# First attention scores ahead of the last projection tiles, head normalisation in two parts, and four smaller moves

## The chip, the cores and the metric

One core of one Trainium2 chip runs the whole program. The metric is the device time of one execution, in microseconds (us). All arithmetic is fp32. The core has TensorE (PE, matrix products and transposes), VectorE (DVE), ScalarE (ACT), GpSimd (POOL) and SyncE (SP), whose queue issues the loads of the weights. Each engine works through its own queue in order; a wait at the head of a queue holds back all that is queued behind it.

## The reference

A residual stream x of 256 tokens by 1024 channels goes through two blocks.

```python
def first_block(x, ...):            # two layers
    x = gated_post_add(x, swiglu_ffn(modulate_pre(x, ...), w_in, w_out), ...)      # 1024 -> 2 x 2816 -> 1024
    x = gated_post_add(x, short_conv_mixer(...) or nsa_mixer(...), ...)            # layer 0: conv, layer 1: nsa
    x = gated_post_add(x, swiglu_ffn(...), ...)

def second_block(x, c, ctx, c_ctx, ...):   # two layers, 256 tokens of x and, in layer 0, 256 of ctx beside them
    # layer 0: differential attention, 8 heads of 2 x 64, keys = ctx and x
    a = softmax(q1 k1) - lam * softmax(q2 k2);  o = rmsnorm(a @ v, subln) * 0.8;  y = o @ w_out
    x = x + g1 * y;  x = x + g2 * swiglu(modulate(rmsnorm(x), ...), w_gu, w_down)   # and the same for ctx
    # layer 1: grouped-query attention, 8 query heads, 2 key heads of 128, only x is carried on
```

A matrix product of fp32 numbers is made here of three products in a faster format: each operand is split into a high part (a copy, rounded) and a low part (what is left), and hi x hi, hi x lo and lo x hi are added in PSUM.

## The kernel before, in words

The program is a list of eleven stages, `subs` 0 to 10: ffn, conv, ffn, kv, ffn, nsa, ffn (256 tokens each), then diff (stage 7) and ffn (stage 8) with 512 tokens, gqa (stage 9, queries for 256 tokens, keys for 512) and ffn (stage 10, 256 tokens). Every engine has its program written out by hand, and semaphores tie them together: `t.done(ins, sem, label)` marks an instruction, `wait_ge(sem, t.at(label))` waits for it.

Weights stream in as units of 128 x 2048 (1 MB) through a ring of three. For each unit SP loads `stage`, ACT copies it to `w_hi` (`split`, L839), DVE subtracts to get `w_lo` (`split`, L1291). A stage has `units` for its first product and `bsteps` for its second, the `down` phase (L2104), in which PE makes all token tiles of one unit at a time, but tile by tile for the last two. The activations of the down phase lie in `mid` and are split piece by piece: piece j by ACT (`mid_split`, L864, marks `mhi_done`) and then by DVE (L1300, marks `mlo_done`), and PE's `ready(j)` waits for that and for the unit's `w_lo`. In the loop over the down steps ACT and DVE run `turn_over(j)`: `mid_split(j + 1)`, then `split` of the unit two ahead. In `nsa` and `gqa` PE writes the gate vector into two PSUM banks after its step 1 (`gate`, L2072), and ACT's copy of them (L1020) stands in `turn_over(0)`.

**diff and gqa** (`Wide`): the projection of 12 or 6 units goes through `rows_product` (L2181 to L2183), one 128-token tile at a time. ACT evacuates (L1119), squares (L1124) and takes roots (L1129) for the norms of q and k, DVE sums, scales and rotates them (L1698 to L1718), PE transposes the result two units later ("ut", L2371), and ACT evacuates that ("evu", L1137). A transposition i waits for evu i - 1, since both use banks 4 and 5. Then come the jobs of the attention (32 in diff, 16 in gqa): scores (L2388, L2391), the maximum on DVE (L1738, L1774, "neg"), the exponential on ACT (L1159, L1193, "exp"), scaling on DVE ("p"), transposition on PE (L2401, "jt"), evacuation on ACT, product with v on PE (L2415, L2418, "pv"). In diff, scores of job J go to banks 2 (J mod 2) and the next, and score J waits for exp J - 2.

**The end of diff**: after the last product ACT copies and squares the last head (L1170, L1174); DVE sums it, forms all 32 means, ACT takes one root over them (L1176), DVE one reciprocal (L1761) and scales the eight heads (L1766, "on"); PE transposes them (L2430, "ot"), ACT evacuates them to `mid` (L1180, "evo"), with `mid_split(0)` after head 3. The second half of the gate copies stands ahead of the eight heads.

**The context half of gqa**: the tokens 256 to 511 are needed from unit 4, tile 2 on. Their modulated activations are made in eight pairs of 128 x 256: DVE's `affine_pair` (L1456) from PSUM, ACT's `hi_pair` (L928), POOL's `lo_pair` (L801). DVE and ACT do all eight at unit 3 of the projection.

**The ffn with 512 tokens** (stage 8): the first piece of its down phase lies, as `h_hi` and `h_lo` slot 0, where chunks 0 and 1 of the up phase's activations were, so `mid_split(0)` waits for the end of the up phase, and PE's `down` waits for all of `mid`.

## Time and profile before

| | us |
|---|---|
| median of 3 runs | 2168.22 |
| lowest, highest | 2164.18, 2172.76 |
| profiled execution, its own time | 2161.73 |
| its span | 2160.0 |
| PE busy in the span | 2059.1 (95%) |
| DVE, ACT, POOL busy | 1380.7, 935.2, 102.5 |

The profiled execution lies 6.5 us below the median of the runs. "Granted clock" is the share of its full rate of 2.4 GHz that TensorE was given in a stretch; it shows two levels, 1.00 (2.4 GHz) and 0.50 (1.2 GHz). A row of the timeline gives start, duration, engine, line, operation and shapes; in brackets the idle time of the engine before it and who ended that.

### The profile page before, as it was taken

The numbers are of one execution on the slowest core, as the hardware profiler recorded it, in microseconds if no ns is written. First come the engines' busy times: TensorE is split into PE (matmuls) and PEld (weight loads), VectorE is DVE, ScalarE is ACT, GpSimd is POOL, SyncE is SP. The second block draws the span as 40 slices with busy tenths as digits, with TensorE's granted clock in tenths as the row PEclk, the third lists the DMA queues.
The fourth block names the chain that finished last, engine by engine and source line by source line (L and its number), as shares of the span: only waits on it lengthen the run. The fifth ranks groups of instructions, "written<-read, shape, count | busy, mean of one in ns | idle before, by whom it ended". The sixth has DMA issues, their size and how long they took to land.

```text
span 2160.0 us, 33553 instructions
## 1 busy us (share of the span) xinstructions
PE 2059.1 (95%) x13545; PEld 1820.7 (84%) x13545; DVE 1380.7 (64%) x1930; ACT 935.2 (43%) x1405; POOL 102.5 (5%) x150
## 2 busy tenths in 40 slices
PE   5999999999899999889999999999999999899999
PEld 3998898998799976459988997688888788868997
DVE  3768798687868784547865755857455335756444
ACT  4345435344633454444355435843222324454343
POOL 2000000000100001200001000010000001100000
PEclk8999999999999998999999999999999999999999
DMA  9897676887688856756855321024435232315553
GB/s 335 271 314 279 230 291 216 294 304 258 214 274 276 319 168 222 264 177 233 284 178 173 98 98 40 1 101 148 160 124 170 78 108 71 125 59 192 179 175 117
DMA packets 246616, 411.38 MB, mean 190 GB/s; under 512 B 10236, under 2 KB 191957, under 8 KB 246485
## 3 DMA queue, kind: packets, MB, share of 16 engines
q1 hardware_dynamic: 245888, 409.31, 55.2%
q8 instruction: 93, 1.52, 0.3%
q10 hardware_dynamic: 597, 0.23, 0.0%
q14 instruction: 38, 0.31, 0.0%
HBM read 408.47 MB, written 1.05 MB: 190 GB/s over the span
## 4 chain that ended last, share of the span: by engine, by line
PE 79%; DVE 9%; ACT 4%; DMA 4%; issue 2%; SPq 1%; POOL 1%; DVEq 0%; ACTq 0%
PE bank L2104 19%; PE bank L2004 14%; PE bank L2006 14%; PE bank L2005 14%; PE bank L2181 2%; PE bank L2183 2%; PE bank L2182 2%; DVE w_lo L1291 2%; DMA ada<-in_ada_w 2%; DVE gate_b L1338 1%; PE bank L1950 1%; DMA stage<-in_ffn_w_in 1%; ACT w_hi L839 1%; PE bank L1974 1%; PE bank L2388 1%
## 5 line engine op out<-in xcount | busy, mean ns | idle before, releaser
L1291 DVE TENSOR_TENSOR w_lo<-stage,w_hi 128x2048 fp32r<-128x2048 f32 x255 | 583.2, 2293 | 438.5 <-ACT w_hi L839 438.0
L839 ACT CAST w_hi<-stage 128x2048 fp32r<-128x2048 f32 x255 | 486.2, 1908 | 628.4 <-PE bank L2104 211.5
L2004 PE MATMUL bank<-h_hi,w_hi 128*128 128x256 f32 (+1 forms) x2336 | 698.1, 299 | 2.6 <-ACT mid L1035 2.6
L2005 PE MATMUL bank<-h_lo,w_hi 128*128 128x256 f32 (+1 forms) x2336 | 695.4, 298 | 0.0
L2006 PE MATMUL bank<-h_hi,w_lo 128*128 128x256 f32 (+1 forms) x2336 | 695.4, 298 | 0.0
L2004 PEld LDWEIGHTS bank<-h_hi,w_hi 128*128 128x128 f32 x2336 | 447.6, 192 | 16.0 <-issue 3.6
L2005 PEld LDWEIGHTS bank<-h_lo,w_hi 128*128 128x128 f32 x2336 | 447.7, 192 | 12.3
L2006 PEld LDWEIGHTS bank<-h_hi,w_lo 128*128 128x128 f32 x2336 | 447.4, 192 | 12.5
L2104 PE MATMUL bank<-w_hi,h_hi 128*128 128x512 f32 x776 | 244.9, 393 | 9.4 <-DVE h_lo L1300 7.9
L2104 PE MATMUL bank<-w_lo,h_hi 128*128 128x512 f32 x776 | 243.8, 391 | 0.0
L2104 PE MATMUL bank<-w_hi,h_lo 128*128 128x512 f32 x776 | 243.3, 391 | 0.0
L1338 DVE SCALAR_TENSOR_TENSOR gate_b<-ada,cond,gate_b 128x1024 f32<-128x1024 f32 x182 | 231.8, 1283 | 5.5
L2104 PEld LDWEIGHTS bank<-w_hi,h_hi 128*128 128x128 f32 x776 | 144.6, 189 | 41.4 <-issue 9.1
L2104 PEld LDWEIGHTS bank<-w_hi,h_lo 128*128 128x128 f32 x776 | 146.6, 189 | 30.8
L2104 PEld LDWEIGHTS bank<-w_lo,h_hi 128*128 128x128 f32 x776 | 146.4, 189 | 30.8
L2181 PE MATMUL bank<-w_hi,h_hi 128*128 128x256 f32 (+1 forms) x552 | 159.4, 289 | 7.5 <-POOL h_lo L801 6.2
L2183 PE MATMUL bank<-w_hi,h_lo 128*128 128x256 f32 (+1 forms) x552 | 157.8, 286 | 0.0
L2182 PE MATMUL bank<-w_lo,h_hi 128*128 128x256 f32 (+1 forms) x552 | 157.8, 286 | 0.0
L1234 ACT ACTIVATE silu_t<-bank 128x256 f32<-128x256 f32 (+1 forms) x132 | 53.2, 417 | 205.6 <-PE bank L2006 191.2
L1823 DVE TENSOR_TENSOR mid<-silu_t,bank 128x256 f32 (+3 forms) x132 | 60.4, 463 | 98.7 <-PE bank L2006 97.4
L2181 PEld LDWEIGHTS bank<-w_hi,h_hi 128*128 128x128 f32 x552 | 107.9, 196 | 8.2 <-POOL h_lo L801 6.7
L2182 PEld LDWEIGHTS bank<-w_lo,h_hi 128*128 128x128 f32 x552 | 108.0, 196 | 0.0
(256 smaller groups left out, 2019.8 us busy)
## 6 DMA issues: line engine op xcount, KB each, us to landing
ada<-in_ada_w SPq DMA_DIRECT2D x114, 1024.0 KB, 6.0
stage<-in_ffn_w_in SPq DMA_DIRECT2D x88, 1024.0 KB, 9.1
stage<-in_ffn_w_out SPq DMA_DIRECT2D x44, 1024.0 KB, 5.1
stage<-in_ffn_w_gu SPq DMA_DIRECT2D x44, 1024.0 KB, 5.2
stage<-in_ffn_w_down SPq DMA_DIRECT2D x22, 1024.0 KB, 5.0
stage<-in_a_w_in SPq DMA_DIRECT2D x12, 1024.0 KB, 7.9
stage<-in_diff_w_in SPq DMA_DIRECT2D x12, 1024.0 KB, 5.2
ada<-in_kv_ada_w SPq DMA_DIRECT2D x8, 1024.0 KB, 5.7
```

Of the source, the lines that this page charges most:

```text
L839: a.copy(w_hi[:, s, :], stage[:, s, :]).then_inc(hi_done, 1)
L1234: a.activation(silu_t[:, q, 0:T], bank[up_bank(s, j, i) + q][:, 0:T], ACT.Silu).then_inc(silu_done, 1)
L1291: v.tensor_tensor(w_lo[:, s, :], stage[:, s, :], w_hi[:, s, :].bitcast(F32), ALU.subtract).then_inc(lo_done, 1)
L1338: ins = v.scalar_tensor_tensor(out=acc[c], in0=w, scalar=cond[:, b, kk, c:c + 1], in1=acc[c], op0=ALU.mult, op1=ALU.add)
L1823: v.tensor_tensor(mid[:, bass.ds(o, T)], silu_t[:, q, 0:T], bank[up_bank(s, j, i) + 2 + q][:, 0:T], ALU.mult).then_inc(mid_done, 1)
L2004: m.matmul(dst[:, 0:T], wh, h_hi[:, h0:h0 + T], start=(k == ks[0]), stop=False)
L2005: m.matmul(dst[:, 0:T], wh, h_lo[:, h0:h0 + T], start=False, stop=False)
L2006: ins = m.matmul(dst[:, 0:T], wl, h_hi[:, h0:h0 + T], start=False, stop=(k == ks[-1]))
L2104: ins = m.matmul(y_bank(T, tt, h)[:, :], a_[:, r:r + P], w_[:, slot, kc * D + h * 512:kc * D + (h + 1) * 512], start=first and n == 0, sto ...
L2181: m.matmul(dst, h_hi[:, r], w_hi[:, slot, c], start=(k == ks[0]), stop=False)
L2182: m.matmul(dst, h_hi[:, r], w_lo[:, slot, c], start=False, stop=False)
L2183: ins = m.matmul(dst, h_lo[:, r], w_hi[:, slot, c], start=False, stop=(k == ks[-1]))
```

## The change

1. **nsa and gqa**: ACT's copies of the gate stand in `turn_over(1)`, behind `mid_split(2)` and the `split` of down unit 3.
2. **diff, start of the attention**: scores 0 and 1 stand ahead of the four tiles of the last projection unit, in banks 4 to 7 (`d_bank`), exps 0 and 1 ahead of its evacuations; scores 2 and 3 wait for no exp.
3. **diff, end**: heads 0 to 6 are summed, rooted and inverted ahead of head 7, whose own chain stands among the scalings. ACT's `mid_split(0)`, the second half of the gate copies and the root of head 7 stand ahead of evo 2.
4. **Stage 8**: ACT makes the first piece once PE has used chunk 1 in its last up product (mark "freed"), DVE makes it ahead of its last product; PE waits for all of `mid` only ahead of token tile 2.
5. **gqa, context half**: the eight affine pairs stand on ACT, three at unit 1, three at unit 2, two at unit 3, each followed by its hi_pair.
6. **gqa, start of the attention**: the last two transpositions ("ut" 3 and 4) stand ahead of tiles 1 and 2 of unit 5, scores 0 and 1 ahead of its tile 3, exps 0 and 1 ahead of ACT's evacuation of its second half.

The core of the diff:

```diff
+        def d_bank(J):
+            return 2 * (J % 2) + (4 if J < 2 else 0)
...
# ACT, mid_split
+                if s["T"] == 512 and s["kind"] == "ffn" and j == 0 and i is None:
+                    act.wait_ge(pe_s, t.at((f"s{s['n']}", "freed")))
+                    act.wait_ge(mid_done, s["c"] + 2)
+                elif s["T"] == 512 and s["kind"] == "ffn" and j == 1:
+                    act.wait_ge(w_used, u - 1)
+                    act.wait_ge(mid_done, s["c"] + 2 * s["bsteps"])
...
# ACT, late_pairs
+            def late_pairs(s, ks):
+
+                tag, c = f"s{s['n']}", s["cs"][1]
                 act.wait_ge(w_used, s["u"])
+                for k in ks:
+                    if pairs_late(s):
+                        for tt in (2 * c, 2 * c + 1):
+                            act.wait_ge(pe_s, t.at((tag, "tr", tt, k // 4)))
+                        act.wait_ge(pool_s, t.at((tag, "lo", k, s["cs"][0])))
+                        t.done(a.activation(h32_pair(k), xt_pair(c, k), ACT.Identity, scale=modc[:, s["A"], 8 * c + k:8 * c + k + 1],
+                                            bias=modv[:, mv(s, 0), 8 * c + k:8 * c + k + 1]), act_s, (tag, "h32", k, c))
+                    hi_pair(s, k, c)
...
# ACT, wide_act
+                        if w.diff and n == s["units"] - 1:
+                            diff_exp(tag, 0)
+                            diff_exp(tag, 1)
                         for half in halves:
+                            if not w.diff and n == 5:
+                                if half == 0:
+                                    turned(w.nk - 2)
+                                else:
+                                    turned(w.nk - 1)
+                                    gqa_exp(tag, 0)
+                                    gqa_exp(tag, 1)
...
-                            if n == 3 and pairs_late(s):
-                                late_pairs(s)
+                            if 0 < n < 4 and pairs_late(s):
+                                late_pairs(s, s["ks"][3 * n - 3:3 * n])
                             act.wait_ge(dve_s, t.at((tag, "rmean", n)))
...
# ACT, diff_act
+                    if J == len(jobs) + 1:
+                        root(0, 28)
...
-                act.wait_ge(dve_s, t.at((tag, "omean")))
-                t.done(a.activation(ada_row[:, 64:96], ada_row[:, 32:64], ACT.Sqrt, scale=1.0 / P), act_s, (tag, "oroot"))
-                gate(s, tag, 1)
                 for h in range(8):
+                    if h == 2:
+                        mid_split(s, 0)
+                        gate(s, tag, 1)
+                        root(28, 32)
                     act.wait_ge(pe_s, t.at((tag, "ot", h)))
                     t.done(a.activation(mid[:, h * 512:(h + 1) * 512], bank[h % 4][:, :], ACT.Copy, scale=SUBLN), act_s, (tag, "evo", h))
-                    if h == 3:
-                        mid_split(s, 0)
...
# ACT, turn_over
-                    if j == 0 and i is None and s["kind"] in ("nsa", "gqa"):
+                    if j == 1 and i is None and s["kind"] in ("nsa", "gqa"):
                         gate(s, tag, 0)
...
# DVE, wide_dve and diff_dve
-                    if n == 3 and pairs_late(s):
-                        late_pairs(s)
...
+                means(0, 28)
+                inverses(0, 28)
                 for h in range(8):
+                    if h == 4:
+                        osum(7)
+                        means(28, 32)
+                    if h == 7:
+                        inverses(28, 32)
...
# DVE, last step of the up phase
+                            if q and j == 10 and T == 512:
+                                mid_split(s, 0)
...
# PE, down
-                if T == 512 and s["kind"] == "ffn":
-                    pe.wait_ge(mid_done, s["c"] + 2 * s["bsteps"])
...
+                        if s["kind"] == "ffn" and T == 512 and i is None and j == 0 and tt == 2:
+                            pe.wait_ge(mid_done, s["c"] + 2 * nb)
...
# PE, wide_pe
+                        if w.diff and n == s["units"] - 1:
+                            pe.wait_ge(act_s, t.at((tag, "evu", w.nk - 1)))
+                            scores(0)
+                            scores(1)
                         for tt in order:
                             half = tt // 2
+                            if not w.diff and n == 5:
+                                if tt in (1, 2):
+                                    turned(w.nk - 3 + tt)
+                                if tt == 3:
+                                    pe.wait_ge(act_s, t.at((tag, "ev", 4, 1)))
+                                    pe.wait_ge(act_s, t.at((tag, "evu", w.nk - 1)))
+                                    scores(0)
+                                    scores(1)
...
-                    if 0 <= i < w.nk:
+                    if 0 <= i < (w.nk if w.diff else w.nk - 2):
+                        turned(i)
...
-                        if J >= 2:
+                    if 2 <= J < len(jobs):
+                        if not w.diff or J >= 4:
                             pe.wait_ge(act_s, t.at((tag, "exp", J - 2)))
```

`turned(i)` is the transposition of unit i (on PE) or its evacuation (on ACT), moved into a function; `scores`, `diff_exp`, `gqa_exp`, `root`, `means` and `inverses` hold what stood in the loops before.

## Rows read from the trace of the kernel before

**Rows 1.** The page, part 4: the chain that ended last, by engine.

```profile
PE 79%; DVE 9%; ACT 4%; DMA 4%; issue 2%; SPq 1%; POOL 1%; DVEq 0%; ACTq 0%
```

**Rows 2.** Waits of PE, whole span: us in total, times, longest us.

```profile
PE bank L2104 <- DVE h_lo L1300: 7.9, 5, 2.5
PE bank L2181 <- POOL h_lo L801: 6.2, 2, 5.7
```

**Rows 3.** Timeline of PE, gates, stage 8, diff and gqa: start us, us.

```profile
956.56 0.70 PE L2104 MATMUL bank<-w_hi,h_hi 128*128 128x512 f32 x2 [2.06 <-DVE h_lo L1300]
960.57 0.70 PE L2104 MATMUL bank<-w_hi,h_hi 128*128 128x512 f32 x2 [1.04 <-DVE h_lo L1300]
...
1321.95 1.99 PE L2388 MATMUL bank<-mid,ada 64*128 64x512 f32 x8 [0.72 <-ACT mid L1119]
1325.88 0.70 PE L2388 MATMUL bank<-mid,ada 64*128 64x256 f32 x4 [1.94 <-ACT gate_b L1159]
...
1397.10 6.64 PE L2430 MATMUL bank<-ident,ada 128*128 128x128 f32 x32 [2.88 <-DVE ada L1766]
...
1702.87 0.70 PE L2104 MATMUL bank<-w_hi,h_hi 128*128 128x512 f32 x2 [2.48 <-DVE h_lo L1300]
...
1891.90 1.12 PE L2391 MATMUL bank<-mid 128*128 128x512 f32 x2 [0.92 <-ACT mid L1193]
...
1942.09 0.85 PE L2104 MATMUL bank<-w_hi,h_hi 128*128 128x512 f32 x2 [2.13 <-DVE h_lo L1300]
```

**Rows 4.** Busy time by stretch: length, PE, PEld, DVE, ACT, POOL, granted clock, DMA, GB/s.

```profile
955.00:962.00 7.00, 4.40 (x18) 3.41 (x19) 5.17 (x5) 4.82 (x5) 0.00 (x0) 1.00 0.63 240
1328.00:1331.40 3.40, 3.40 (x11) 1.51 (x11) 2.62 (x6) 2.33 (x9) 0.00 (x0) 0.51 0.00 0
1396.50:1403.00 6.50, 5.90 (x28) 5.93 (x29) 5.23 (x9) 4.58 (x8) 0.00 (x0) 0.50 0.00 0
1703.50:1706.90 3.40, 3.40 (x10) 2.62 (x9) 2.37 (x2) 3.17 (x3) 0.00 (x0) 0.51 0.03 7
1864.00:1870.60 6.60, 5.81 (x27) 5.81 (x28) 6.00 (x15) 0.38 (x1) 0.73 (x1) 0.50 0.00 0
1942.60:1945.90 3.30, 3.30 (x9) 2.55 (x9) 2.92 (x4) 2.66 (x3) 0.00 (x0) 0.50 0.32 127
```

**Rows 5.** The same view over the stretches of the gqa projection.

```profile
1864.80:1873.20 8.40, 8.40 (x48) 8.40 (x49) 5.20 (x14) 0.00 (x0) 0.00 (x0) 0.64 0.25 66
1873.60:1885.20 11.60, 11.60 (x99) 11.60 (x98) 7.68 (x10) 5.18 (x8) 0.00 (x0) 1.00 0.07 29
```

**Rows 6.** Timeline of ACT and DVE in gqa.

```profile
1851.80 0.21 ACT L1129 ACTIVATE astat<-astat 128x4 f32<-128x4 f32 x1 [3.09 <-DVE astat L1700]
...
1877.80 0.63 ACT L1137 COPY mid<-bank 128x256 f32<-128x256 f32 x2
...
1881.42 0.69 DVE L1718 TENSOR_TENSOR mid<-silu_t 128x512 f32<-128x512 f32 x1
```

**Rows 7.** One line's instructions: ns minimum/median/maximum, first and last start us.

```profile
L1063 ACT ACTIVATE mid<-bank,q_scale x8: 473/475/476, 807.0 to 826.6; 128x256 f32<-128x256 f32 x8
L928 ACT CAST h_hi<-mid x48: 391/407/411, 1123.7 to 1860.9; 128x256 fp32r<-128x256 f32 x48
L1300 DVE TENSOR_TENSOR h_lo<-mid,h_hi x82: 681/685/1226, 168.5 to 2142.8; 128x512 fp32r<-128x512 f32 x67, 128x1024 fp32r<-128x1024 f32 x15
L1433 DVE TENSOR_TENSOR h_lo<-mid,h_hi x6: 1455/1457/1459, 241.6 to 1960.6; 128x512 fp32r<-128x512 f32 x6
L793 POOL TENSOR_TENSOR h_lo<-mid,h_hi x53: 450/732/2774, 35.7 to 1965.2; 128x256 fp32r<-128x256 f32 x27, 128x128 fp32r<-128x128 f32 x18, 128x512 fp32r<-128x512 f32 x8
```

**Rows 8.** Timeline of ACT at the end of diff.

```profile
1394.01 0.63 ACT L1174 ACTIVATE silu_t<-ada 128x512 f32<-128x512 f32 x1
...
1395.75 1.06 ACT L1020 COPY gate_b<-bank 128x512 f32<-128x512 f32 x2
...
1401.37 1.04 ACT L864 CAST h_hi<-mid 128x1024 fp32r<-128x1024 f32 x1
```

More of the change, by code:

```diff
@@ L1099, in wide_act, with turned @@
                 w, u = Wide(s), s["u"]
+                def turned(i):
+                    act.wait_ge(pe_s, t.at((tag, "ut", i)))
+                    for c in range(2):
+                        k = w.tiles(i) * P
+                        if w.diff and i == 0 and c == 0:
+                            act.wait_ge(*ring_free(rv(s["v"] - 1) * VEC_UNITS + 3))
+                        ins = a.copy(w.dest(i, c), bank[4 + c][:, 0:k])
+                    t.done(ins, act_s, (tag, "evu", i))
                 if w.diff:
@@ L1130, in wide_act @@
                     i = n - 2
-                    if 0 <= i < w.nk:
-                        act.wait_ge(pe_s, t.at((tag, "ut", i)))
-                        for c in range(2):
-                            k = w.tiles(i) * P
-                            if w.diff and i == 0 and c == 0:
-                                act.wait_ge(*ring_free(rv(s["v"] - 1) * VEC_UNITS + 3))
-                            ins = a.copy(w.dest(i, c), bank[4 + c][:, 0:k])
-                        t.done(ins, act_s, (tag, "evu", i))
+                    if 0 <= i < (w.nk if w.diff else w.nk - 2):
+                        turned(i)
                 if w.diff:
@@ L1902, in _ @@
                     wide_dve(s, tag)
-                if s["kind"] in ("diff", "gqa") or T == 512:
+                if s["kind"] in ("diff", "gqa"):
                     mid_split(s, 0)
@@ L1975, in acc_sum, with cols_product @@
                 ins.then_inc(ada_sum, 1)
-            def cols_product(s, dst, slot, q, first=False):
+            def cols_product(s, dst, slot, q, first=False, last=False):
                 T, ks = s["T"], s["ks"]
@@ L2006, in cols_product @@
                     ins = m.matmul(dst[:, 0:T], wl, h_hi[:, h0:h0 + T], start=False, stop=(k == ks[-1]))
+                    if last and k == 1:
+                        t.done(ins, pe_s, (f"s{s['n']}", "freed"))
                 return ins
@@ L2332, in wide_pe, with turned, scores @@
                 w, u = Wide(s), s["u"]
+                def turned(i):
+                    pe.wait_ge(dve_s, t.at((tag, "rope", i)))
+                    if i:
+                        pe.wait_ge(act_s, t.at((tag, "evu", i - 1)))
+                    for c in range(2):
+                        for tt in range(w.tiles(i)):
+                            o = tt * WCOL + c * P
+                            ins = m.transpose(bank[4 + c][:, tt * P:(tt + 1) * P], w.nat(i)[:, o:o + P], ident[:, :])
+                    t.done(ins, pe_s, (tag, "ut", i))
+                def scores(J):
+                    h, tt, k0 = jobs[J]
+                    if w.diff:
+                        for m_ in range(2):
+                            r = slice(64 * m_, 64 * m_ + 64)
+                            ins = m.matmul(bank[d_bank(J) + m_][:, 0:(4 - k0) * P], w.qT[r, h, tt * P:(tt + 1) * P],
+                                           w.kT[r, h, k0 * P:512], start=True, stop=True)
+                    else:
+                        ins = m.matmul(bank[J % 2][:, :], w.qT[:, h, tt * P:(tt + 1) * P], w.kT[:, h // 4, :], start=True, stop=True)
+                    t.done(ins, pe_s, (tag, "s", J))
+                jobs = diff_jobs if w.diff else gqa_jobs
                 def context_part(n):
@@ L2363, in wide_pe @@
                     i = n - 2
-                    if 0 <= i < w.nk:
-                        pe.wait_ge(dve_s, t.at((tag, "rope", i)))
-                        if i:
-                            pe.wait_ge(act_s, t.at((tag, "evu", i - 1)))
-                        for c in range(2):
-                            for tt in range(w.tiles(i)):
-                                o = tt * WCOL + c * P
-                                ins = m.transpose(bank[4 + c][:, tt * P:(tt + 1) * P], w.nat(i)[:, o:o + P], ident[:, :])
-                        t.done(ins, pe_s, (tag, "ut", i))
+                    if 0 <= i < (w.nk if w.diff else w.nk - 2):
+                        turned(i)
                 n = s["units"] - 1
@@ L2481, in up_step @@
                                     pe.wait_ge(mid_done, c + 2 * (j - 1) + q + 1)
-                            ins = cols_product(s, bank[banks[part] + q], n % RING, q, first and part == 0 and q == 0)
+                            ins = cols_product(s, bank[banks[part] + q], n % RING, q, first and part == 0 and q == 0,
+                                               s["kind"] == "ffn" and T == 512 and i is None and j == 10 and part == 1 and q == 1)
                             ins.then_inc(w_used if q else part_done[part], 1)
```

86 lines of the change are left out of this document (40 added, 46 removed).

## Prediction

> **What bounds the kernel now.** The chain of the page comes first: 79% of it is PE's [rows 1], and PE is busy for 95% of the span. So a microsecond counts only where PE stands still, or runs at the lower clock, and the change has to be read at those places. PE's waits are read next, with the timeline of PE for the time of each [rows 2, 3]: the reader is to see six gaps at the places that the change touches, 2.06 and 1.04 us behind the gate of nsa, 0.72 and 1.94 us at the start of diff's attention, 2.88 us ahead of the transpositions that end diff, 2.48 us between up and down phase of stage 8, 5.7 us in the projection of gqa, 2.13 us behind the gate of gqa. Third, the busy time by stretch [rows 4]: behind five of these places PE has a granted clock of 0.50 (the 1.2 GHz level) for 3.3 to 6.6 us, though it is busy. Only behind the 2.06 us of nsa the clock stayed at 1.00. A gap of over 2 us thus mostly costs about half of such a stretch on top of itself.
>
> **The change part by part.** The terms are savings of PE time, against the profiled execution's own 2161.7 us.
>
> *Gate copies (1).* In turn_over(0) ACT waited for PE's gate, and behind that wait in its queue stood mid_split 2, which PE needs first after the gate, and the split of unit 3. With the copies one turn later, piece 2 and w_hi, w_lo of unit 3 are made while PE is still in steps 0 and 1 (11 us), and only piece 3 (0.6 us on ACT, 0.69 us on DVE) stands behind the copies; PE needs it after twelve products of 512 columns, 2.8 us at twice the 0.12 us of a product of 256 (96 of them took 11.6 us [rows 5]), so it is hidden. What is queued behind the moved copies is that piece alone; the gate itself is read by the residual update, after the down phase. SP issues nothing new; its next load waits for w_lo of unit 3 and starts earlier. nsa: 2.06 + 1.04 = 3.1 us [rows 3] (2.1 if the second gap stays). gqa: 2.13 us, and half of the 3.3 us at clock 0.50 behind it [rows 3, 4], 1.65: 3.8 us (2.1 without the clock).
>
> *Start of diff's attention (2).* Scores 0 and 1 cost 1.9 us of PE before and after [rows 3], so moving them is free. Their maxima and exps (about 5 us of DVE and ACT) fall into unit 11, 11.6 us of PE as unit 5 of gqa [rows 5], in which both engines are nearly idle. After the unit PE waits 0.72 us for its evacuation as before, then runs scores 2 and 3. Unit 11 ended at 1321.2; with the scores it ends at 1323.1, score 2 starts at 1323.8 instead of 1325.88 [rows 3]: 2.1 us. Then the stretch at clock 0.51 [rows 4], which followed the gap of 1.94 us: it can go with the gap. A job waits for DVE and ACT too, so between nothing and half of the 3.4 us, 1.7, is to be had; PE is busy for all of the stretch, which is nearer to the upper end, and I take 1.1. Sum 3.2 us, from 1.9 to 3.8.
>
> *End of diff (3).* DVE can scale heads 0 to 3 from about 1392.5 on. PE's heads 0 and 1 follow the gate at 1394.2. But head 2 goes into a bank of the second gate half, and ACT now copies that half behind evo 0, evo 1 and mid_split 0. From the end of the last square at 1394.64 [rows 8]: two evos 0.6 + 0.6 with 0.2 of handing over, the piece 1.04, the copies 1.06: 1398.2. PE so waits 3.1 us between heads 1 and 2, where it waited 2.88 us before head 0 [rows 3]. The clock then most likely falls as it did [rows 4], and the six heads left take 6.64 / 8 = 0.83 us each [rows 3], to 1403.2, with DVE's first piece long done; before, the down phase started at 1403.8. That is 0.6 us, and up to 0.5 us of the down phase falls into the low stretch: I take 0.3 us. At full clock heads 2 to 7 would be bound by ACT (0.6 each) and end at 1400.8: 3.0 us. The bounds are -0.5 and 3.0.
>
> *First piece of stage 8 (4).* ACT's copy (1.04) and DVE's subtraction (1.23 [rows 7]) fit in the 18 products of 0.23 us, 4.2 us, that are left after chunk 1; both engines idle there. DVE's last product stands behind its piece and is not late, since it waits for PE's end anyway. Saved: 2.48 us [rows 3] and half of 3.4 us [rows 4], 1.7: 4.2 us (2.5 without the clock). Piece 1 still waits for the end of the up phase; it takes ACT and DVE under 4 us, while step 0 is 11 us of PE: hidden. The wait for all of mid ahead of tile 2 comes 5.5 us into it.
>
> *Context half of gqa (5).* The 5.7 us wait for POOL's last piece [rows 2] goes, if POOL is done when PE comes to tile 2 of unit 4, at 1858.9. One pair on ACT is 0.475 + 0.407 us [rows 7]. Three pairs are 2.65 us, two 1.8 us, and ACT idled 3.09 us ahead of its root, at unit 1 and again at unit 2 [rows 6]: hidden. At unit 3 the two pairs end at 1857.4, POOL 0.7 to 1.5 us later, about when PE comes. Without the wait the second half of unit 4 also runs at full clock: 48 products took 8.40 us, while 96 take 11.6 in unit 5 [rows 5], so 5.8: 2.6 us. Together 8.3 us at the end of unit 4. DVE loses eight operations and gains an overlap: POOL's pieces now meet w_lo subtractions. A DVE subtraction beside a POOL one took 1.457 instead of 0.685 us, and a POOL one up to 2.77 us instead of 0.73 [rows 7]: one waits for the other. Each of three meetings costs DVE from nothing to 0.8 us; PE stands 0.5 us from needing DVE's results. I take 0.6 us off: 7.7 us; the bounds are 4 and 8.3.
>
> The Trainium skill, GPSIMD Engine Reference, section Key points, says that GpSimd shares its SBUF interfaces with VectorE and contends with VectorE instructions that have two SBUF inputs. By that rule the pieces speak against this place, and the trace agrees in kind (the 1.457 us). If each of the eight pieces held DVE up for all of its 0.73 us, an estimate of 5.8 us, gqa would give 2 us here and the forecast would be 2150.
>
> *Start of gqa's attention (6).* Count from the end of unit 4, 1873.2 before [rows 5]. PE's tile 0 of unit 5 ends at +3.3 with the transposition before it. Transposition 3 must wait for evu 2, which stands in ACT's queue behind the root of unit 4: it ended at 1878.43 [rows 6], +5.2. A new stall of 1.9 us. Transposition 3 (0.4) and tile 1 (2.9) end at +8.5; transposition 4 needs DVE's rotation, done at 1882.1 [rows 6], +8.9; with it (0.9), tile 2, two scores (0.9), tile 3 PE is at +16.5, and score 2 follows the evacuation at +17.2. Before it started at 1891.90 [rows 3], +18.7. Gain 1.5 us; if the clock falls after the 1.9 us, as it did after 1.94 us, -0.2 us or less, -1.8 at worst.
>
> Sum: 3.1 + 3.8 + 3.2 + 0.3 + 4.2 + 7.7 + 1.5 = **23.8 us**, 1.1%. On the profiled execution that gives 2137.9. The median of the runs lies 6.5 us higher, and I take the saving off that: **2144 us**. All terms at their low end give 2.1 + 2.1 + 1.9 - 0.5 + 2.5 + 4 - 1.8 = 10.3, at their high end 3.1 + 3.8 + 3.8 + 3.0 + 4.2 + 8.3 + 1.5 = 27.7.
>
> **The rivals.**
> *A, DVE and POOL in each other's way.* If DVE loses 1 us at unit 1 and another at unit 2, ACT's root and so evu 0 come 2.3 us late, PE waits ahead of transposition 1, and a low stretch (1.7 us) follows: gqa's term falls from 9.2 to about 4. For it: the 1.457 us. Against: POOL took the longer waits in the rows. Saving 18 us: 2150.
> *B, the clock stays up at the end of diff.* Gap 3.1 against 2.88 speaks against it. Saving 26.5: 2142.
> *C, the time is given back further on.* If the loads of the 256-token ffn stages paced them, an earlier start would end in a wait for weights. PE has no wait for a load behind nsa at all, so little speaks for it. Only the last three places would count in part; saving under 10 us: 2160.
> *D, slower: the low clock over the attentions.* New, shorter gaps could keep PE low through diff's 75 us and gqa's 37 us of attention. By my value the stretch of 3.4 us cost 1.1 us, 0.33 per us: 37 us for 112, less the 23.8: 2181. It decides from about 105 us of low clock on. Against it: the trace has no other low stretch in either attention, and they have fewer gaps afterwards.
>
> **How the numbers follow.** About 0.5% (10.8 us) is what a measurement of this kernel can tell from no change. The forecast's own case has a chance of 0.70 (2138 to 2150), A 0.14, B 0.07, C 0.05, D 0.04. Faster: 0.70 + 0.14 + 0.07, less some executions that lie high: 0.89. Same 0.07, slower 0.04. The range takes in A, B and the ends of the costs: from 2161.7 - 27.7 to 2168.2 - 10.3, that is 2134 to 2158.
>
> **What would show it.** Right: no wait for POOL in gqa and clock 1.00 over units 4 and 5; no gap between up and down phase of stage 8, and none behind the gates; a gap of about 3 us between heads 1 and 2 at the end of diff, and one of about 2 us in unit 5 of gqa. Wrong: a wait ahead of transposition 1 of gqa, POOL pieces or w_lo subtractions there well over their usual length, clock 0.50 in new places, a wait for weights in the stage behind.

## The result, and the profile of the changed kernel

| | before | changed |
|---|---|---|
| median of 3 runs, us | 2168.22 | 2140.71 |
| lowest, highest, us | 2164.18, 2172.76 | 2136.26, 2147.65 |
| profiled execution, its own time, us | 2161.73 | 2147.65 |

The ratio is 0.9873, with a 95% interval of 0.983 to 0.9915: faster by 27.5 us, where 2144 (2134 to 2158) was forecast. Two later series of the changed kernel, experiments e7b and e11 below, gave 0.9901 (0.9881 to 0.9921) and 0.9901 (0.9881 to 0.9922). The median of its 13 executions is 2144.84 us.

The chain of the page, by engine, now has more of PE and no POOL (before: [rows 1]).

```profile
PE 80%; DVE 10%; ACT 4%; DMA 3%; issue 2%; SPq 1%; POOL 0%; DVEq 0%; ACTq 0%
```

Of PE's waits by line and releaser (us in total, times, longest), two are new. Those of [rows 2] are gone but for 0.2 us on DVE and 0.5 us on POOL, neither at a place of the six edits. The new ones:

```profile
PE bank L2398 <- ACT mid L1123: 3.3, 2, 1.8
...
PE bank L2505 <- ACT gate_b L1036: 3.0, 1, 3.0
```

PE's timeline at the places of [rows 3], in the changed kernel (start, duration, operation, idle time before it and its releaser):

```profile
963.86 1.03 PE L2130 MATMUL bank<-ident,modc 128*128 128x128 f32 x8
964.65 0.70 PE L2160 MATMUL bank<-w_hi,h_hi 128*128 128x512 f32 x2
...
1316.73 1.99 PE L2406 MATMUL bank<-mid,ada 64*128 64x512 f32 x8
...
1331.19 1.13 PE L2406 MATMUL bank<-mid,ada 64*128 64x256 f32 x8 [0.77 <-ACT mid L1155]
1333.73 1.13 PE L2406 MATMUL bank<-mid,ada 64*128 64x512 f32 x4 [0.82 <-ACT mid L1182]
...
1401.77 4.20 PE L2505 MATMUL bank<-ident,ada 128*128 128x128 f32 x24 [3.02 <-ACT gate_b L1036]
1405.62 1.10 PE L2160 MATMUL bank<-w_hi,h_hi 128*128 128x512 f32 x2
...
1702.14 0.39 PE L2062 MATMUL bank<-h_hi,w_lo 128*128 128x512 f32 x1
1702.37 0.62 PE L2160 MATMUL bank<-w_hi,h_hi 128*128 128x512 f32 x2
...
1851.50 0.63 PE L2398 MATMUL bank<-ident,mid 128*128 128x128 f32 x4 [1.52 <-ACT mid L1123]
...
1868.77 0.63 PE L2398 MATMUL bank<-ident,mid 128*128 128x128 f32 x4 [1.82 <-ACT mid L1123]
1872.37 1.09 PE L2398 MATMUL bank<-ident,mid 128*128 128x128 f32 x8
1876.17 1.88 PE L2409 MATMUL bank<-mid 128*128 128x512 f32 x4
1881.64 1.10 PE L2409 MATMUL bank<-mid 128*128 128x512 f32 x2 [0.72 <-ACT mid L1155]
...
1928.63 1.03 PE L2130 MATMUL bank<-ident,modv 128*128 128x128 f32 x8
1929.42 0.70 PE L2160 MATMUL bank<-w_hi,h_hi 128*128 128x512 f32 x2
```

The reader is to see the first product of the down phase right behind the gate's transpositions (L2130) in nsa and gqa, and right behind the last product of the up phase (L2062) in stage 8; the 3.02 us gap, now between heads 1 and 2 at the end of diff; and in gqa no wait on POOL, but 1.52 us ahead of transposition 1 and 1.82 us ahead of transposition 3. The busy time by stretch (columns as [rows 4]) shows the clock at 1.00 at these places, but for the end of diff and the last row, a stretch of nsa's attention that no edit touches:

```profile
964.60:971.60 7.00, 7.00 (x34) 5.80 (x33) 3.71 (x5) 4.56 (x8) 0.00 (x0) 1.00 1.04 384
1333.00:1336.40 3.40, 2.67 (x18) 1.79 (x20) 3.31 (x7) 2.81 (x11) 0.00 (x0) 1.00 0.00 0
1402.70:1406.30 3.60, 3.60 (x20) 3.50 (x19) 1.19 (x2) 3.27 (x6) 0.00 (x0) 0.55 0.02 5
1851.00:1867.00 16.00, 15.45 (x128) 15.27 (x128) 13.76 (x27) 9.70 (x16) 2.31 (x3) 1.00 0.39 143
1868.70:1872.10 3.40, 3.33 (x28) 3.32 (x28) 3.33 (x6) 2.27 (x3) 0.00 (x0) 1.00 0.12 43
1926.00:1934.00 8.00, 8.00 (x41) 6.71 (x40) 3.76 (x4) 3.40 (x4) 0.00 (x0) 1.00 1.04 393
...
912.00:921.00 9.00, 9.00 (x44) 5.30 (x40) 3.02 (x22) 2.29 (x10) 1.82 (x2) 0.50 0.39 133
```

To place the time, I cut each trace at waits of PE that every kernel here has: m1, the wait of 2.3 us at the boundary ahead of nsa's kv stage (798 us); m2, the 4.0 us at the boundary behind nsa (974 in before); m3, the 1.47 us at 1122; m4, the 1.20 us ahead of the last pair of products of diff's attention (1390); m5, the 0.65 us at the boundary behind diff (1457); m6, score 2 of gqa (1892); m7, the 2.15 us at the boundary behind gqa (1960). Lengths in us, each from one profiled execution:

| kernel | own time | m1-m2 | m3-m4 | m4-m5 | m5-m6 | m6-m7 |
|---|---|---|---|---|---|---|
| before | 2161.73 | 175.64 | 267.83 | 67.06 | 434.63 | 68.14 |
| before, again (e12) | 2173.78 | 184.53 | 268.92 | 66.92 | 433.48 | 67.75 |
| changed | 2147.65 | 182.60 | 264.69 | 65.56 | 422.23 | 64.11 |
| changed, again (e7b) | 2144.55 | 177.53 | 264.49 | 63.91 | 423.40 | 64.13 |
| changed, again (e11) | 2141.41 | 176.73 | 264.36 | 63.92 | 422.23 | 64.11 |
| four places put back (e1) | 2154.47 | 175.98 | 268.96 | 63.92 | 427.82 | 68.09 |
| two further edits (e8b) | 2140.00 | 174.68 | 264.27 | 62.96 | 421.40 | 64.12 |
| three further edits (e10) | 2137.95 | 174.92 | 264.55 | 62.98 | 420.39 | 64.11 |

The two first profiles differ by 14.1 us, not 24: between m1 and m2 the changed one is 7.0 us longer, though its gate there costs 3.6 us less (from the gate's transpositions to m2 17.12 us, before 20.70). The other 10.5 us are low clock in nsa's attention: over m1-m2 the granted clock was 0.82 on average, in before 0.88, and PE was busy for 164.6 us instead of 154.6.

### The profile page after: what moved, and what is told of

Its sections match the earlier page's. It is cut to its first block, busy times and chain, and to the rows that moved or that the text cites. A ratio compares the mean times of both kernels' runs of the same rounds, so it can differ in the third digit from the quotient of the medians.

```text
span 2145.9 us, 33562 instructions
## 1 busy us (share of the span) xinstructions
PE 2060.0 (96%) x13545; PEld 1820.0 (85%) x13545; DVE 1377.7 (64%) x1925; ACT 939.0 (44%) x1414; POOL 104.6 (5%) x150
## 3 DMA queue, kind: packets, MB, share of 16 engines
q8 instruction: 93, 1.52, 0.3%
HBM read 408.47 MB, written 1.05 MB: 191 GB/s over the span
## 4 chain that ended last, share of the span: by engine, by line
PE 80%; DVE 10%; ACT 4%; DMA 3%; issue 2%; SPq 1%; POOL 0%; DVEq 0%; ACTq 0%
PE bank L2160 19%; PE bank L2060 14%; PE bank L2062 14%; PE bank L2061 14%; PE bank L2239 2%; PE bank L2241 2%; PE bank L2240 2%; DVE w_lo L1335 2%; DVE gate_b L1382 1%; PE bank L2006 1%; DMA ada<-in_ada_w 1%; DMA xs<-in_ada_w 1%; PE bank L2030 1%; ACT w_hi L842 1%; PE bank L2406 1%
## 5 line engine op out<-in xcount | busy, mean ns | idle before, releaser
L2062 PE MATMUL bank<-h_hi,w_lo 128*128 128x256 f32 (+1 forms) x2336 | 695.4, 298 | 0.0
L2062 PEld LDWEIGHTS bank<-h_hi,w_lo 128*128 128x128 f32 x2336 | 447.4, 192 | 12.5
```

Of the source, the lines that this page charges most:

```text
L2062: ins = m.matmul(dst[:, 0:T], wl, h_hi[:, h0:h0 + T], start=False, stop=(k == ks[-1]))
```

## The experiments

**Is each part worth what its place shows?** e1 puts four places back; of its edit, the gates and the order of stage 8 and of diff's scores:

```
-                    if j == 1 and i is None and s["kind"] in ("nsa", "gqa"):   # ACT: gate copies
+                    if j == 0 and i is None and s["kind"] in ("nsa", "gqa"):
...
-                            if q and j == 10 and T == 512:                       # DVE: first piece of stage 8
-                                mid_split(s, 0)
...
-                        if w.diff and n == s["units"] - 1:                       # PE, ACT: scores 0, 1 early
-                            scores(0)
-                            scores(1)
```

> The changed kernel with four of its places put back as they were: the gate copies of nsa and of gqa at turn-over 0, the start of diff's attention (scores 0 and 1 behind the last unit), and the first piece of stage 8 behind the last product. The end of diff and both gqa projection parts stay. Theory (each part is worth what its own place shows, independent of the others): against the changed kernel the marks of the trace fall back by 3.6 us at the gate of nsa, 3.1 at the start of diff's attention, 4.4 at stage 8 and 4.0 at the gate of gqa, 15 us together; the gaps of 2.06 and 1.04, of 1.94, of 2.48 and of 2.13 us stand there again, and the low clock behind three of them. Rival (what one place gives another takes back, or the places share their low clock): under 10 us together. A second question: the stretch of nsa's attention, which no part touches, had more low clock in the changed kernel's profile (10 us longer). If that comes with the changed program it is here too; if it comes with the single execution, this profile may have it or not.

One execution took 2154.47 us. All four gaps stand there again (2.06 and 1.03, 1.94, 2.49, 2.13 us). Two of them:

```profile
1702.32 0.70 PE L2151 MATMUL bank<-w_hi,h_hi 128*128 128x512 f32 x2 [2.49 <-DVE h_lo L1335]
...
1934.68 0.70 PE L2151 MATMUL bank<-w_hi,h_hi 128*128 128x512 f32 x2 [2.13 <-DVE h_lo L1335]
```

From the gate to m2 it needs 20.73 us, 3.6 more than the changed kernel. The start of diff (m3-m4) costs 4.3 us, more than the 3.1 by which the first profiles differ: the low clock behind the gap lasts 6.8 us here, as in e12, instead of 3.4 [rows 4]. Stage 8 costs 4.4 (m5 to the first transposition of gqa: 388.59 against 384.22) and the gate of gqa 4.0 (m6-m7). Together 16.3 us against the 15 expected: what these four places give is not taken back at another. All four were undone at once, none of them alone. The rest of m5-m6, 1.2 us, is a stretch of low clock behind the 1.82 us gap of gqa, which the changed kernel's first profile does not have. The stretch of nsa is a short one in this execution, 175.98 us with the old place of the gate copies.

**What holds DVE in gqa?** In the changed kernel DVE's round per unit is 6.85 us where it was 6.31, and evacuation 0 so comes 1.1 us later. DVE and POOL there:

```profile
1840.13 2.29 DVE L1335 TENSOR_TENSOR w_lo<-stage,w_hi 128x2048 fp32r<-128x2048 f32 x1
1842.33 0.68 DVE L1740 TENSOR_REDUCE astat<-mid 128x4 f32<-128x512 f32 x1
1843.04 0.69 DVE L1742 TENSOR_SCALAR astat<-astat 128x4 f32<-128x4 f32 x1
...
1846.99 2.29 DVE L1335 TENSOR_TENSOR w_lo<-stage,w_hi 128x2048 fp32r<-128x2048 f32 x1
```

```profile
1841.12 1.89 POOL L804 TENSOR_TENSOR h_lo<-mid,h_hi 128x256 fp32r<-128x256 f32 x1 [13.90 <-ACT h_hi L937]
...
1842.97 1.42 POOL L804 TENSOR_TENSOR h_lo<-mid,h_hi 128x256 fp32r<-128x256 f32 x2
```

The scaling of four elements took 0.69 us, where it takes 0.17 elsewhere. It ran beside POOL's second piece and ended 0.02 us behind it (the two of the last row start at 1842.97; the second piece ends at 1843.71). POOL's first piece took 1.89 us instead of 0.73: it began inside w_lo and ended 0.6 us after it. e2 cuts POOL's pieces to 16 of their 256 columns and leaves the rest of these low parts out:

```
-                t.done(g.tensor_tensor(dst, h32_pair(k), hi, ALU.subtract), pool_s, (tag, "lo", k, c))
+                src = h32_pair(k)
+                if pairs_late(s) and c == s["cs"][1]:
+                    dst, src, hi = dst[:, :, 0:8], src[:, :, 0:8], hi[:, :, 0:8]
+                t.done(g.tensor_tensor(dst, src, hi, ALU.subtract), pool_s, (tag, "lo", k, c))
```

> The changed kernel, but each of POOL's eight late subtractions in gqa covers 16 of its 256 columns; the rest of the context half's low parts is left out. It asks what made DVE's period per unit 6.85 instead of 6.31 us. Theory A (POOL's pieces hold DVE): the small scaling of four elements, 0.69 us beside POOL, takes 0.17 again, DVE's period is 6.3 us, and the wait of PE ahead of transposition 1 falls from 1.52 to about 0.5 us: 1.0 us less. Rival (ACT's late pairs delay the root): DVE's period stays at 6.8 us and the wait at 1.5 us, since ACT's work is the same.

Its scaling, over all of the kernel (ns minimum/median/maximum):

```profile
L1745 DVE TENSOR_SCALAR astat<-astat x13: 170/174/175, 1205.4 to 1868.6; 128x16 f32<-128x16 f32 x8, 128x4 f32<-128x4 f32 x4, 128x8 f32<-128x8 f32 x1
```

The round is 6.30 us and the wait ahead of transposition 1 is 0.45 us, 1.07 less (before had 0.46); m5-m6 is 421.18, 1.05 shorter. ACT's work is the same, so it is POOL that holds DVE. e3 takes DVE's scaling away instead, in gqa alone:

```
...
+                            else:
+                                t.done(a.activation(flat_astat[:, 32:32 + k], flat_astat[:, 0:k], ACT.Sqrt, scale=1.0 / P, bias=stat[:, 31:32]), act_s, (tag, "rroot", n))
...
+                        if w.diff:
+                            dve.wait_ge(dve_s, t.at((tag, "rsum", n)))
+                            t.done(v.tensor_scalar(flat_astat[:, 16:16 + k], flat_astat[:, 0:k], 1.0 / dh, EPS, ALU.mult, ALU.add), dve_s, (tag, "rmean", n))
```

> The changed kernel, but in gqa the root takes the scale and the added constant itself (as its scale and bias), so that DVE's scaling of the means, the one operation that grew from 0.17 to 0.69 us beside POOL, is gone. Theory 1 (the loss sits in that one operation): DVE's period falls from 6.85 to about 6.1 us and PE's wait ahead of transposition 1 to 0.3 us or less, 1.2 us or more saved. Theory 2 (whatever DVE does beside POOL's piece is held up): the next operation takes over the 0.5 us, the period is about 6.6 us, the wait about 1.1 us, 0.4 us saved.

```profile
1830.32 0.69 DVE L1754 TENSOR_TENSOR mid<-mid,astat 128x512 f32<-128x512 f32 x1
1831.04 1.12 DVE L1762 TENSOR_TENSOR silu_t<-mid,gate_b 128x512 f32<-128x512 f32 x1
1832.08 0.41 DVE L1763 TENSOR_TENSOR silu_t<-mid,gate_b 128x256 f32<-128x256 f32 x1
```

Theory 2 in kind: a later operation of the round now loses 0.43 us (1.12 instead of 0.69) and the round is 6.61 us. But the loss has moved behind the root, so evacuation 0 is not held: the wait is 0.54 us, 0.98 less, where theory 2 expected a wait of 1.1 us, and m5-m6 is 0.9 us shorter (421.37). This kernel's execution took 2133.30 us, that of e4 below 2149.80, with at most 1 us between their edits: 13.5 of the 16.5 us lie between m1 and m2.

**Was it the spreading or the engine?** e6b spreads the eight scale-and-shift operations as the change does, but leaves them on DVE:

```
...
+                    if 0 < n < 4 and pairs_late(s):                      # DVE, ahead of the sums of unit n
+                        for kk in s["ks"][3 * n - 3:3 * n]:
+                            affine_pair(s, kk, s["cs"][1])
```

> The changed kernel, but the eight scale-and-shift operations of gqa's context half, spread over units 1 to 3 as 3, 3 and 2, are done on DVE as before, 0.46 us each, ahead of each unit's sums. It asks whether the spreading alone gives the gain, or the engine. Theory (ACT had room and DVE had none): DVE's period at units 1 and 2 grows from 6.85 to about 8.2 us, PE's wait ahead of transposition 1 from 1.52 to about 2.9 us, another wait of 1 us or more ahead of transposition 2, perhaps low clock behind it: gqa's projection takes 2.5 to 5 us longer than in the changed kernel. Rival (the spreading is what counts): within 0.7 us of the changed kernel there.

```profile
1851.79 1.08 PE L2395 MATMUL bank<-ident,mid 128*128 128x128 f32 x4 [3.82 <-ACT mid L1117]
```

DVE's round is 8.03 us, the wait 3.82 us, and the clock is at 0.50 from 1849.9 to 1856.6. The second wait that was expected, ahead of transposition 2, is not there, but m5-m6 is 4.5 us longer (426.74). Spreading alone gives less than half of the 7.5 us; the rest needs the idle ACT.

**The wait in unit 5 of gqa.** e4 takes ACT's queue away as its cause:

```
+                            if not w.diff and n == 4:
+                                turned(2)                                 # ACT, ahead of the root
                             act.wait_ge(dve_s, t.at((tag, "rmean", n)))
```

> The changed kernel, but in gqa ACT copies out transposition 2 ahead of the root of unit 4, in the 1.49 us in which it waits for DVE. Theory (ACT's queue is only the first of two reasons): the wait of 1.82 us ahead of transposition 3 goes down to 0.3 us or less, but transposition 4 needs DVE's rotation of unit 4, and PE now waits 1.5 to 2 us for that ahead of tile 2: nothing saved (within 0.3 us). Rival (the queue was the bound): 1.5 us saved, no new wait on DVE.

```profile
1869.66 0.63 PE L2400 MATMUL bank<-ident,mid 128*128 128x128 f32 x4
...
1874.96 1.09 PE L2400 MATMUL bank<-ident,mid 128*128 128x128 f32 x8 [1.80 <-DVE mid L1762]
```

The 1.82 us ahead of transposition 3 are gone and 1.80 us stand ahead of transposition 4; m5-m6 is 422.24, in the changed kernel 422.23. Nothing is saved. So the chain through DVE has to be shortened, which e9 does:

```
+                            if n == 4 and tt == 3 and not w.diff:
+                                turned(2)                                 # PE, inside unit 4
...
+                            if not w.diff and n == 4 and half == 0:       # ACT: square of the first half
+                                a.activation(w.sq[:, 0:512], w.nat(4)[:, 0:512], ACT.Square)
```

> The changed kernel, but in gqa transposition 2 stands ahead of tile 3 of unit 4 instead of behind the unit, its evacuation ahead of that of unit 4, and ACT squares unit 4 in two halves, so that the first half is copied and squared while PE is still in tile 3. Experiment e4 put the bound of unit 5 at DVE's rotation of unit 4, which follows the square. Theory (the chain ACT copy, square, DVE sums and rotation of unit 4 is the bound): the square ends about 1.1 us earlier, counted from the end of unit 4, the wait of 1.82 us ahead of transposition 3 is gone, a wait of about 0.7 us on DVE stands ahead of transposition 4, and score 2 comes 1.1 us earlier (0.7 to 1.5). Rival (transposition 2 stalls PE inside unit 4, since evacuation 1 or rotation 2 is late there): a new wait of over 0.5 us inside unit 4 takes the gain back.

```profile
1858.14 0.60 PE L2405 MATMUL bank<-ident,mid 128*128 128x128 f32 x4
...
1868.93 1.09 PE L2405 MATMUL bank<-ident,mid 128*128 128x128 f32 x8 [1.14 <-DVE mid L1767]
```

Transposition 2 does not wait inside unit 4, the wait on DVE is 1.14 us (0.7 was expected), and from transposition 1 to score 2 there are 29.16 us instead of 30.14: 0.98 saved.

**The gap at the end of diff.** e5b changes the order on ACT:

```
+                gate(s, tag, 1)
                 for h in range(8):
                     if h == 2:
+                        root(28, 32)
                         mid_split(s, 0)
-                        gate(s, tag, 1)
-                        root(28, 32)
```

> The changed kernel, but at the end of diff ACT copies the second gate half ahead of evo 0 and 1, and takes the root of head 7 and the first piece behind them. Theory (the 3.02 us gap between heads 1 and 2 is ACT's order alone): the bank of head 2 is free at about the end of the last square plus 1.1 us, the gap falls to 0.6 to 0.8 us, DVE's first piece ends the wait of the down phase, and the down phase starts 2.1 us earlier (1.5 to 2.5), with up to 0.5 us more if the low clock behind the gap goes too. Rival (what follows is bound elsewhere: eight evos on ACT at 0.63 us or the scaling on DVE): the gap goes, but the down phase starts less than 0.7 us earlier, with new waits of PE between heads 4 and 7.

```profile
1398.23 2.15 PE L2505 MATMUL bank<-ident,ada 128*128 128x128 f32 x16 [0.55 <-ACT gate_b L1036]
1401.21 1.21 PE L2505 MATMUL bank<-ident,ada 128*128 128x128 f32 x8 [0.83 <-DVE ada L1820]
1402.37 0.70 PE L2160 MATMUL bank<-w_hi,h_hi 128*128 128x512 f32 x2
```

From m4 to the down phase it takes 9.58 us. That is 2.2 less than the 11.77 of the changed kernel's first profile, but that one has low clock there; against e7b and e11, which like e5b have none, it is 0.9 less (10.51), not the 2.1 of the theory. Head 2 starts 2.5 us earlier, and 1.5 of them are lost again: from head 2 to the down phase it takes 4.14 us instead of 2.60, with a new wait of 0.83 us ahead of head 6. The rival expected such a wait, but less than 0.7 us of gain; the result lies between the two. m4-m5 is 62.95: 2.6 us less than in the first profile, 1.0 less than in those of e7b and e11.

The row puts the new wait down to DVE. But DVE had scaled head 6 by 1400.27, and in the program head 6 also waits for evacuation 2, whose bank it takes. That one stood in ACT's queue behind the first piece and ended at 1401.07, 0.02 us ahead of DVE's last scaling (head 7), which the row names:

```profile
1399.44 1.05 ACT L873 CAST h_hi<-mid 128x1024 fp32r<-128x1024 f32 x1
1400.39 0.68 ACT L1231 ACTIVATE mid<-bank,stat 128x512 f32<-128x512 f32 x1
...
1400.40 0.69 DVE L1820 TENSOR_TENSOR ada<-ada,ada_row 128x512 f32<-128x512 f32 x1
```

So it is again ACT's order, as read from the program and these rows; no run moved the piece.

**Times, and the stretch of nsa.** e7b is the changed kernel again, e8b has the edits of e3 and e5b, e10 those and the edit of e9, e11 is the changed kernel beside e10, e12 the kernel before.

> The changed kernel as it is, timed again beside the kernel before. Theory (the parts' marks add up to 24.5 us, and the rest of what one profile shows is the clock over nsa's attention, which differs between executions): ratio 0.9887 (24.5 of 2168), within 0.984 to 0.992. Rival (the median of the first runs, 27.5 us, is the size): 0.987 or less with an interval that leaves 0.9887 out. The profile's marks from 1130 us on lie as in the first profile within 1 us once the start of the stretch is subtracted; only the stretch of nsa's attention and the low clock behind boundaries may differ.

Measured: 2146.31 us (2144.55 to 2148.86), ratio 0.9901 (0.9881 to 0.9921). The interval holds the theory's 0.9887, so the rival falls.

> The changed kernel with two further edits: the gate copies first at the end of diff, and the root of gqa with its scale and constant on ACT, so that DVE's small scaling beside POOL's pieces is gone. Theory (both waits were real and lie at separate places): 2.1 + 1.0 = 3 us less than the changed kernel, a ratio against the kernel before lower by 0.0014; the interval of the times can't resolve that, the marks of the trace can: down phase of diff 2.1 us earlier, transposition 1 of gqa 1.0 us earlier. Rival (the gain is given back at the next boundary): the marks behind gqa lie less than 1.5 us earlier, reckoned from the start of diff.

Measured: 2139.11 us (2134.72 to 2140.00), ratio 0.9857 (0.9837 to 0.9878). The marks give 0.96 us between m4 and m5 against e7b, 2.6 against the first profile of the changed kernel, and 0.8 between m5 and m6 (against 422.23). Where the clock stays up, the two edits together are thus worth 1.8 us, not the 3 expected. The times differ by 7.2 us, more than the marks explain.

> The changed kernel with three further edits together: gate copies first at the end of diff, the root of gqa with scale and constant on ACT, transposition 2 of gqa ahead of tile 3 of unit 4. Theory (separate places, all of it on PE's path): 2.1 to 2.6 at the end of diff, 0.9 and 1.1 in gqa, 4.1 to 4.6 us less than the changed kernel, a ratio to the kernel before of about 0.9875 if the changed kernel's is 0.9895. Rival (the low clock over nsa's attention decides more than that): the two intervals of this call overlap, though the marks show the 4 us.

Measured: 2137.95 us (2131.71 to 2140.58), ratio 0.9854 (0.9832 to 0.9877). m5-m6 is 420.39, 1.84 shorter, just the 0.86 of e3 and the 0.98 of e9 together. m4-m5 is 62.98, 0.9 shorter than in e11, where 2.1 to 2.6 were expected. The three edits thus give 2.8 us by the marks, not 4.1 to 4.6; the medians differ by 8.4. This version has the lowest median here, and its interval lies just below that of the changed kernel:

> The changed kernel as it is, on the same chip as the run before, to have both against the same runs of the kernel before. Theory: ratio 0.989 (0.987 to 0.991); where the end of diff shows no low clock, the stretch from the last pair of products to the boundary is 63.9 us long, where it does, 65.6; the same for 12.9 or 14.1 us from transposition 3 to the third score of gqa.

Measured: 2146.31 us (2140.08 to 2149.72), ratio 0.9901 (0.9881 to 0.9922). Its profile has no low clock at either place, with 63.92 us and 12.87 us from transposition 3 to score 2, as expected for that case.

> The kernel before as it is, for a second profile of it. The stretch from the start to the end of nsa's attention and down phase (between two fixed marks at about 798 and 974 us) took 175.6 us in its first profile, and 170.4 to 183.8 us in eleven profiles with the gate copies moved, where 172.0 would answer to the first profile (3.6 us less for the gate). Theory (executions differ there, whatever the kernel, and the first profile of before was a short one, as its own time, 6.5 us under the median, says): the profiled time less that stretch is again 1986 us within 2 us, however long the stretch is, and it is more likely longer (median of the other profiles 177.8 plus 3.6, 181 us) than 176. Rival (moving the gate copies itself lengthens nsa's attention by some 6 us): the stretch is 174 to 177 us again, and the profiled time near 2162 us, far from the kernel's median of 2168.

Measured: 2173.78 us; the stretch m1-m2 took 184.53, so the rival, which had it at 174 to 177 again, falls. What is left of the time is 1989.3 us, 3.2 more than in the first profile and 1.3 more than the theory allowed: 1.3 us lie ahead of m1, 1.4 between m2 and m3, 1.1 in the longer low clock between m3 and m4, and others of opposite sign behind them. With 3.6 us off for the gate, the two profiles of before have 172.0 and 180.9 us between m1 and m2; the eleven with the gate copies moved have 170.4 to 183.8. So a lengthening by 6 us is not seen. One of a few us is not ruled out: only three profiles have the old place of the copies (e1's stretch is 172.4 us on the same count).

## Why the prediction was right, point by point

| term | forecast (bounds), us | measured, us |
|---|---|---|
| gate of nsa | 3.1 (2.1 to 3.1) | 3.6 |
| gate of gqa | 3.8 (2.1 to 3.8) | 4.0 (3.6 against e12) |
| start of diff | 3.2 (1.9 to 3.8) | 3.1; 4.2 to 4.6 against e12 and e1 |
| end of diff | 0.3 (-0.5 to 3.0) | 1.5; 3.1 where the clock stays up |
| stage 8 | 4.2 (2.5 to 4.2) | 4.4 |
| gqa, context half | 7.7 (4 to 8.3) | 7.5 (6.4 against e12) |
| gqa, start of attention | 1.5 (-1.8 to 1.5) | 0.5; -0.7 where the clock falls |
| sum | 23.8 (10.3 to 27.7) | 24.6 |

The measured column is the difference of the first two profiles, cut at the marks; e1 confirms four of its rows by undoing them. The median of 13 executions lies 23.4 us under the first median of before. The 27.5 us of the first three runs are 3 us more than the marks, the 21.8 and 22.8 us of the medians of e7b and e11 2 to 3 us less; the kernel's executions differ by 13.5 us among themselves. That the sum of the marks is only 0.8 us off the forecast is in part luck: 1.2 us too little at the end of diff, 0.9 too little at the gates and stage 8, 1.0 too much at the start of gqa's attention and 0.2 in its context half.

*Gates.* Right in mechanism, 0.5 us short in nsa. Two gaps of 3.10 us cost 3.58, 0.24 each beside the idle time. An estimate from the rows gives the same: the pairs of products in the down phase follow each other every 0.46 us while each record lasts 0.62, so a gap reckoned from a record's end is 0.16 too short; and the first pair behind a gap takes 0.70, 0.08 more. The forecast took only idle time and clock, so nsa, gqa (4.0) and stage 8 (4.4) all lie above their upper bounds. Piece 3 behind the moved copies was hidden, as the clock of 1.00 and a busy PE from 964.6 to 971.6 show.

*Start of diff.* Right in mechanism; the sum is right because two errors cancel. Score 2 was to start 2.1 us earlier; counted from m3 it starts 1.5 us earlier (203.50 to 202.03 us; 1.8 in e11). The clock's share was taken as 1.1 us of a 3.4 us stretch, but from score 2 to m4 the time fell from 64.33 to 62.66 us, 1.7 less, half of the stretch. Where that stretch is 6.8 us long, as in e1 and e12, it is worth about 1 us more.

*End of diff.* The gap came out as worked out (3.02 for 3.1 us). The step that failed was that the clock falls "as it did", with 0.83 us for each of heads 2 to 7. It fell 1.3 us after they began and stayed down for 3.4 us, where it had been down for 6.8 in before, so that they took 3.85 us and not 6 times 0.83. Rival B, which had the clock stay up there and 3.0 us saved, is the case of three of nine profiles with this gap (e1, e7b, e11), and 3.1 us are saved there. The price is right, its working is not: at ACT's 0.6 us each the six heads would have ended at 1401.8 in the forecast's own count, not at 1400.8, and only 2.0 us would have been saved. In e11 they take 2.60 us, 0.43 each, and no wait for ACT stands among them:

```profile
1397.62 2.84 PE L2505 MATMUL bank<-ident,ada 128*128 128x128 f32 x24 [3.02 <-ACT gate_b L1036]
1400.21 0.71 PE L2160 MATMUL bank<-w_hi,h_hi 128*128 128x512 f32 x2
```

*Stage 8.* Right, gap and clock: 2.48 + 1.9 us.

*Context half of gqa.* The sum is right to 0.2 us, and its shape too, a little gained and a little lost. Rival A was right in its place (a wait ahead of transposition 1, DVE late) and wrong in its price: 0.54 us per round and 1.1 us for PE by unit 1, not 2.3, and no low clock behind it. The forecast had 0.6 us off for it. The short operation, not the long one, was held: w_lo kept its 2.29 us, and the price was paid by the scaling of four elements behind it. The Trainium skill (GPSIMD Engine Reference, Key points) puts the contention at instructions of VectorE in a 2-port performance mode or with two SBUF inputs; e2 bears out that the engines hold each other; the held scaling has one input, and whether it ran in such a mode no run shows. By that rule each of POOL's eight pieces could have cost its 0.73 us, where a burst of three cost 0.54 once.

*Start of gqa's attention.* The 1.82 us (1.9 forecast) ahead of transposition 3 and the time of transposition 4 (9.0 us behind the end of unit 4, forecast 8.9) came out. The step that failed is the cost of the two scores: 0.9 us was set down for both, and each costs 0.94 ([rows 3] has 1.12 with its tail for one). That is the missing 1.0 us. The fall of the clock behind the wait (1.7 to 1.8 us), set as possible, came in two of ten profiles (e1, e7b) and cost 1.2 us.

*C and D.* C is out: no wait for a weight stands behind nsa, and with the stretch m1-m2 set aside m7 lies earlier by the full sum (21.1 us from m2 on, and 3.6 for the gate of nsa). D is out: neither attention has new low stretches but those named, and diff's attention takes 62.66 us from score 2 to m4 in every profile with the early scores, within 0.05 us.

*The range* held, but not for the reason given. It was made of costs and bounds of the edits; the spread that showed is in nsa's attention, where PE waits for loads and for the other engines and the clock falls behind some waits and not others. Both profiles of before came from the two ends of that spread (2161.73 and 2173.78). Setting the saving off against the median, not the profiled execution, was right for that reason.

What stays open: why the clock falls behind the same wait in one execution and not in another. The runs show only that it is not the kernel (three profiles of the changed one differ in it), and what a fall costs at each place. And of the 7.2 us by which e8b is faster than e7b, only 1.8 to 3.4 have a place in the marks.

## What to carry to other kernels

Read a change's worth at marks that both traces have, not from two totals: here a stretch with untouched attention in it moved by 10 us, and the parts added up only once it was cut out. When a wait is removed, work out the next one on the same path: taking ACT's queue away gave nothing, since DVE's chain held PE for 1.80 of the 1.82 us, and shortening that chain gave 1.0 us. At the end of diff a gap of 3.02 us went down to 0.55, and only 0.9 us were gained, since the next wait stood right behind. Compare such a place between profiles with the same clock: against one with low clock the gain read 2.2 us. Idle time of an engine can take work only if its neighbours don't pay: work moved onto the idle ACT was free, the same work spread on DVE cost 4.5 us, and POOL's share of it held DVE for 0.5 us a round until the held operation lay behind the critical one.

## What the runs showed of the hardware that I had not expected

A DVE operation of four elements that met POOL's piece ended with it (0.69 instead of 0.17 us), while a subtraction of 2048 columns on DVE kept its 2.29 us, and POOL's piece that began inside it ended only 0.6 us after it (1.89 instead of 0.73 us). The granted clock of TensorE behind a wait of 1.7 to 3.0 us is not a property of the program: behind the 3.02 us gap it fell in six of nine profiles, behind the 1.8 us gap in two of ten. Of the changed kernel's own three profiles one shows the fall at the first place and another at the second. In these eight cases it stayed down for 3.4 us, and that cost 1.2 to 1.7 us; at the start and the end of diff it was down for 6.8 us in some profiles, in nsa's attention for 9 us and more (912 to 921 above).
